# Whole background tiles between the steps of the scans' chain

## The reference, cut to what matters

```python
def chunk_scan(q, k, v, log_a):          # S_t = diag(a_t) S_{t-1} + k_t v_t^T, o_t = S_t^T q_t
    def step(state, inp):
        qc, kc, vc, ac = inp
        cum = jnp.cumsum(ac, axis=2)
        o_inter = jnp.einsum('bhtk,bhkv->bhtv', qc * jnp.exp(cum), state)
        diff = cum[:, :, :, None, :] - cum[:, :, None, :, :]
        decay = jnp.where(causal_in_chunk, jnp.exp(jnp.where(causal_in_chunk, diff, 0.0)), 0.0)
        scores = jnp.einsum('bhtk,bhsk,bhtsk->bhts', qc, kc, decay)
        o_intra = jnp.einsum('bhts,bhsv->bhtv', scores, vc)
...
def bidir_scan(q, k_fwd, k_bwd, v, la_fwd, la_bwd):
    fwd = chunk_scan(q, k_fwd, v, la_fwd)
    bwd = flip(chunk_scan(flip(q), flip(k_bwd), flip(v), flip(la_bwd)))
    return (fwd + bwd).astype(q.dtype)
...
o_b = mixer_hgrn2(b_q, b_ff, b_fb, b_i, b_g, lower_bounds[l], hgrn_norm_g[l])
o_c = mixer_gla(c_q, c_k, c_v, c_g, c_lrf, c_lrb, gla_gate_w2[l], gla_gate_b[l], gla_norm_g[l])
g_a, g_b, g_c = jnp.split(jax.nn.sigmoid(gates), N_BRANCH, axis=-1)
```

## Time and profile before

| | us |
|---|---|
| median of 3 runs | 5423.82 |
| lowest, highest run | 5412.58, 5428.38 |
| profiled execution, time | 5412.35 |
| profiled execution, span | 5410.8 |
| TensorE (PE) busy in the span | 4449.6 (82%) |
| VectorE (DVE) busy | 2012.1 (37%) |
| ScalarE (ACT) busy | 1194.3 (22%) |

### The profile page before, as it was taken

The page is one execution under the profiler, slowest core; times in us unless marked ns, Lnnn a source line. Parts: engine busy times, 40 slices in busy tenths (PEclk is TensorE's granted clock), DMA queues, the critical chain, the costliest instruction groups (busy, mean ns, idle before and its releaser), DMA issues. The chain is left out here.

```text
span 5410.8 us, 54373 instructions
## 1 busy us (share of the span) xinstructions
PE 4449.6 (82%) x20668; PEld 2944.3 (54%) x20668; DVE 2012.1 (37%) x3485; ACT 1194.3 (22%) x2000; POOL 274.2 (5%) x450
## 2 busy tenths in 40 slices
PE   6999998666689699996598997399778877973995
PEld 2365643444444588885397873344356766733442
DVE  0266630333352555554233751400133366514011
ACT  0123310222220100001113751011134424510111
POOL 0000000000000000000031000011000000000111
PEclk9899999888899799998799998599899989985997
DMA  7101211000021311112223113199500012120996
GB/s 307 51 27 54 72 70 77 19 19 19 0 94 66 125 47 47 47 47 117 96 67 121 37 44 117 41 326 335 171 3 4 2 44 105 42 109 32 321 334 206
DMA packets 104466, 521.96 MB, mean 96 GB/s; under 512 B 15825, under 2 KB 37217, under 8 KB 84593
## 3 DMA queue, kind: packets, MB, share of 16 engines
q1 hardware_dynamic: 70752, 404.86, 20.1%
q0 software_dynamic: 30432, 112.81, 6.5%
q10 hardware_dynamic: 3120, 2.10, 0.1%
HBM read 438.46 MB, written 81.26 MB: 96 GB/s over the span
## 5 line engine op out<-in xcount | busy, mean ns | idle before, releaser
L1700 PE MATMUL scans_G<-ring,hT 128*128 128x512 f32 (+1 forms) x1024 | 394.5, 543 | 6.2 <-ACT scans_stg L1818 6.2
L1700 PEld LDWEIGHTS scans_G<-ring,hT 128*128 128x128 f32 x1024 | 192.8, 191 | 193.5 <-issue 176.0
L2199 PE MATMUL moe_g_ps<-ring,moe_xT 128*128 128x512 f32 x512 | 229.6, 602 | 3.0 <-ACT moe_xT L2253 1.5
L2235 PE MATMUL moe_y_ps<-ring,moe_aT 128*128 128x512 f32 x512 | 225.2, 593 | 1.5 <-issue 1.5
L2199 PE MATMUL moe_u_ps<-ring,moe_xT 128*128 128x512 f32 x512 | 225.0, 592 | 0.0
L153 PE MATMUL mlp_z<-ring_r,mlp_w_high 128*128 128x512 f32 x512 | 200.7, 392 | 22.1 <-DVE ring_r L147 22.0
L154 PE MATMUL mlp_z<-hT_r,mlp_w_high 128*128 128x512 f32 x512 | 199.8, 390 | 0.0
L155 PE MATMUL mlp_z<-ring_r 128*128 128x512 f32 x512 | 199.7, 390 | 0.0
L153 PE MATMUL mlp_y_ps<-mlp_w_high,oN_r 128*128 128x512 f32 x512 | 199.2, 389 | 0.0
L154 PE MATMUL mlp_y_ps<-ring_r,oN_r 128*128 128x512 f32 x512 | 199.2, 389 | 0.0
L155 PE MATMUL mlp_y_ps<-mlp_w_high,oN_r 128*128 128x512 f32 x512 | 199.2, 389 | 0.0
(11 more groups left out here) (499 smaller groups left out, 8672.4 us busy)
## 6 DMA issues: line engine op xcount, KB each, us to landing
ring<-in_w_all SPq DMA_DIRECT2D x126, 2048.0 KB, 8.3
ring<-in_w_mlp SPq DMA_DIRECT2D x16, 2048.0 KB, 7.5
branch_gates<-scans_stg POOLq DMA_DIRECT2D x48, 256.0 KB, 2.3
merge_raw<-branch_gates SPq DMA_DIRECT2D x16, 768.0 KB, 5.2
ring<-in_w_even SPq DMA_DIRECT2D x6, 1536.0 KB, 8.6
norm_moe_x<-x_rows SPq DMA_DIRECT2D x16, 512.0 KB, 7.4
h_rows<-norm_moe_h POOLq DMA_DIRECT2D x16, 512.0 KB, 2.9
diff_w<-in_w_diff POOLq DMA_DIRECT2D x4, 1536.0 KB, 6.6
```

The costliest lines, as they stand in the source:

```text
L1700: ins = pe.matmul(G[:, b % 2, 0:w.shape[2]], m["hT"][:, k, n * P:(n + 1) * P], w[:, k, :], start=k == 0, stop=k == KD - 1)
L2199: ins = pe.matmul(what[:, j % 2, :], xT[:, j % 2, k, :], w[:, k, :], start=k == 0, stop=k == KD - 1)
L2235: ins = pe.matmul(Y[:, half, :], aT[:, j % 2, k, :], w[:, k, half * HALF:(half + 1) * HALF], start=k == 0, stop=k == K4 - 1)
```

## The change

The condition of the loop in `background` is changed. Before, a matmul was put out as long as the background put out so far was less than `us`, so that a call could stop in the middle of a tile. Now a tile that has been started is always finished (`at[1]` is not 0), and a new one is started only if at least half of its cost lies before `us`.

```diff
             def background(us):
 
-                while at[0] < len(TILES) and at[2] < us - 1e-6:
+                while at[0] < len(TILES) and (at[1] or at[2] + 0.5 * COST[TILES[at[0]][0]] < us):
                     b, k = at[0], at[1]
                     what, x, j, n = TILES[b]
                     w = wview(j)
```

## The result

| | before | after |
|---|---|---|
| median, us | 5423.82 (5 runs) | 5453.94 (5 runs) |
| lowest, highest | 5412.58, 5428.38 | 5447.49, 5463.84 |
| ratio of the times, with its 95% interval | | 1.006 (1.0042 to 1.0077) |
| profiled execution, us | 5412.35 | 5459.52 |

The change makes the kernel 30.1 us slower; 5445 was forecast, 21 us slower. The stage, from its first matmul (L1716) to the end of the tail, lasted 732.9 us before and 770.1 after in the profiled executions: 37.2 us more, of their difference of 47.2. The other 10 us lie in stages whose code is the same; executions of one kernel differ by as much.

A forecast was written before the change was run, and what follows sets the result against it. The prediction took TensorE's work plus its idle time to bound the stage. Added idle time of 16.3 us and 5.1 for the clock gave +21.4 on the median of 5423.82, so 5445 us, range 5426 to 5460.

The forecast's parts named there:

- What bounds the stage: End of the scans' stage: TensorE's work plus its idle time; the chain's own length counts for nothing else.
- The lengths of the levels without the clock: Turn 0's eight levels: sum 107.1 us instead of 95.76, so 11.4 us longer.
- The wait ahead of level 1: Turn 0, empty second window of level 0: TensorE waits 5 us before level 1.
- Idle time of 13.1 us in turn 0 and 16.3 in the stage: TensorE's added idle time: 13.1 us in turn 0's levels, 0.9, 1.6 and 0.7 elsewhere in the stage.
- Behind the turns: Between turns: 0.86 us more idle behind turn 0; net +0.7 behind turn 1, where TensorE arrives about 1.2 early.
- The level 4 wait of turn 1: Turn 1, level 4: a lone N tile leaves TensorE 1.6 us idle where none was.
- The clock: Turn 0's levels: three clock falls, one in level 0 and two at 2.8 us gaps, 1.7 us each: +5.1 (0 to +12).
- the third of the rivals: Turn 0: clock falls at nearly every empty window, some seven times 1.7 us; +28 us, 5452; chance 0.20.
- a gain from uncut tiles: Turn 0's levels: pauses come from restarting after cut tiles, about 14 of 15.8 us idle go; 5410; chance 0.04.
- The change is not hidden by ScalarE: Rival for the stage: ScalarE's planned copies hold TensorE, so time stays at 5424 within 5; chance 0.04.
- The clock didn't stay up: Rival for turn 0: clock stays up, +16.3 us or up to 3 less, 5437 to 5440; chance 0.16.
- The total: Whole kernel: 16.3 us without the clock plus 5.1 for the clock, +21.4 us, 5445 against the median.

The follow-up runs named there:

- overfull: Kernel before with 4 and 7 matmuls instead of 2 and 5 planned into turn 0's first and second windows: 5413.42 us against 5423.23.
- filled_more: Changed kernel with useless matmuls in turn 0's empty windows and behind lone N tiles of second windows: 5437.78 us against 5423.23 for the kernel before.
- turns12_whole: Kernel before with whole tiles only in turns 1 and 2, turn 0 as before: 5424.56 us against 5421.59.
- turn0_whole: Kernel before with whole tiles only in turn 0, turns 1 and 2 as before: 5456.17 us against 5421.59.
- tile_per_window: Changed kernel replanned so each window of turn 0's levels gets exactly one tile, with ScalarE's copies and later starts adjusted: 5432.41 us against 5422.66 for before.
- first_empty: Kernel before with all first windows of turn 0 empty, their background moved to the second ones, no whole tiles: 5459.91 us against 5421.59.
- one_empty: Kernel before with only the first window of level 3 in turn 0 empty, its background moved to the second: ratio 1.0011 to before.
- level0_empty: Kernel before with both windows of level 0 in turn 0 empty, the background moved to level 1's first window: ratio 1.0017 to before.
- whole_filled: Changed kernel with useless matmuls in the windows of turn 0 that it leaves empty: 5451.71 us against 5421.59 for the kernel before.
- tuned: Kernel before with 3 and 6 matmuls instead of 2 and 5 planned into turn 0's first and second windows: 5414.15 us against 5422.66.

## Why the prediction was nearly right, point by point

**What bounds the stage**: right. The end is TensorE's work plus its idle time; overfull (levels 14.8 us longer, stage 10.1 shorter) shows it more strongly than any row of before did.

**The lengths of the levels without the clock**: right. Levels 4 and 5, where the clock stays at 1.00, last 12.82 us each for the 12.79 worked out. The predicted sum of 107.1 came out at 109.48 when the windows were filled. The wait ahead of level 1 was said to be 5 us and is 4.97. Idle time of 13.1 us in turn 0 and 16.3 in the stage stands: it is the larger part of the 20.1 us that filled_more keeps, and with the 19.3 and 1.6 us below it makes up the stage's 37.2.

**Behind the turns**: right in sizes that hardly matter. The wait for ScalarE behind turn 0 is 6.02 us, 0.85 more than in the earlier trace rows (0.86 predicted). The other two, from TensorE's timeline after:

```profile
589.72 2.06 PE L1780 MATMUL scans_A<-scans_KQ 64*128 64x128 f32 x32 [1.54 <-DVE scans_KQ L2050]
...
666.61 2.23 PE L1744 MATMUL scans_A<-identity,scans_E 128*128 128x128 f32 x16 [1.32 <-DVE scans_E L1964]
```

The level 4 wait of turn 1 is 1.54 us (1.6 predicted) and the one behind turn 1 is 1.32 (1.2 predicted), at a transpose. The wait of 0.48 us at 628.76 is gone, as predicted.

**The clock**: the step that failed, in size. Counted level by level against the prediction, turn 0 is longer by

| level | 0 | 1 | 2 | 3 | 4 | 5 | 6 | 7 |
|---|---|---|---|---|---|---|---|---|
| predicted, us | 11.89 | 16.21 | 13.85 | 11.95 | 12.79 | 12.79 | 13.82 | 13.82 |
| measured, us | 13.61 | 20.72 | 17.54 | 13.67 | 12.82 | 12.82 | 18.09 | 17.13 |

which sums to 19.3 us, all of it in rows at the low clock. The term was 3 x 1.7 = 5.1, with 12 as its upper bound, and 19.3 lies beyond that bound too. It failed in both factors. The falls are five, not three: level 0 and each of the levels 2, 3, 6 and 7, so all four gaps of 2.8 us and not two. And a fall costs 3.9 us on average, not 1.7: 6.2 for levels 0 and 1 together, 3.7, 1.7, 4.3 and 3.3 for the others. Level 3 is the cheapest, since its slow N tile runs into time that would have been idle. The 1.7 came from the earlier trace rows, where gate tiles of 7 us follow one another without a pause and the clock returns in under 4 us. Here what follows is a group of 2 us and often another gap, and the clock stays low for 6 to 20 us. The row was a right witness that the clock falls and a wrong one for how long. That the work behind the gap makes the difference is argued, not shown: no run puts a long tile straight behind a gap of 2.7 us. The kernel came out near the third of the rivals, which gave +28 us with the remark that slow groups may add to it; measured are +30.1 by the medians, and +37.2 in the stage of the profiled pair. Its factors were off as well: seven falls at 1.7 us, where five at 3.9 were found.

In the stage some 1.6 us are left over: a fall of its own behind the prologue of turn 0, where a product of keys and values takes 3.45 us behind a wait of 2.48. The same wait is in before without a fall. TensorE's timeline before, then after:

```profile
312.75 1.97 PE L1757 MATMUL scans_B<-scans_V,scans_KQ 128*128 128x256 f32 x8 [2.48 <-DVE oN L1975]
...
315.65 3.45 PE L1757 MATMUL scans_B<-scans_V,scans_KQ 128*128 128x256 f32 x8 [2.48 <-DVE oN L1975]
```

The fall stands in the profiles of all five kernels whose prologue holds 32 matmuls, and in one of the seven with 29: turns12_whole, whose order up to there is that of before. So the changed prologue may favour this fall, but isn't needed for it, and its cause stays open. The prediction gave the prologue no price.

The Trainium skill, "TensorE: Matmul & The Clock Gate", section "HAM oscillation — how this bites in real kernels", says that gaps between bursts bring the half level back and that each return costs again. This trace agrees: each of the six gaps of 2.7 us and more in the levels of turn 0 was followed by a group of 2.97 to 3.79 us instead of 2.05. In the forecast I weighed it with the full clock of the earlier trace rows, which stands beside pauses of under 1.4 us and so said nothing of gaps of 2.7. The row at 312.75 above, a wait of 2.48 us at full clock, was nearer; the prediction didn't use it, and it would have pointed the wrong way.

**The refuted rivals**: a gain from uncut tiles doesn't exist; where nothing stands between two groups the second still starts 2.70 us behind the end of the first, which is the selection's time. The change is not hidden by ScalarE either. The clock didn't stay up.

**The total** came near with one term far too small and nothing to make up for it: 16.3 held, and the clock's 5.1 should have been some 14 (30.1 less 16.3) by the medians and 19.3 by the profiled execution. The profiled execution, 5459.52, is 5.6 us above the median of its kernel, and the one of before 11.5 below its own, so the stage's figures lean to the high side. How much the falls vary from run to run was not measured, but turn0_whole is a second sample of the same order in turn 0: its levels last 127.21 us at 0.77, with a fall in level 5 that the kernel after doesn't show and a shorter one in level 6.

## What to carry to other kernels

Where one engine bounds a stage and fills the gaps of a chain, count the time that it stands idle, not the length of the chain: too much in a gap cost nothing on balance here (overfull was 0.15% faster, though its waits for ScalarE's copies rose by 2.3 us), too little costs its length once. Here it cost about as much again through TensorE's clock, at gaps of some 2.7 us between small groups, so price such a gap from a row with the same work around it, not from one between long tiles. If filler must be rounded to whole pieces, rounding up in every gap did better here than rounding to the nearest piece (tile_per_window against after), but it was still 0.16% slower than cut pieces.

## What the runs showed of the hardware

- While groups of 16 matmuls with 32 rows and 128 columns alternated with gaps of 2.8 and 5 us, the clock did not come back: 0.50 from 340 to 360 us in the kernel after. Each fall in its levels lasted 6 to 20 us, against under 4 in the earlier trace rows.
- Every gap of 2.69 us or more ahead of a group in the levels of turn 0 came with a fall: 23 of 23 in after, turn0_whole, first_empty, one_empty and level0_empty, with groups of 2.59 to 3.79 us instead of 2.05. The wait of 2.48 us ahead of L1757 came with one in six profiles of twelve.
- A pause of 1.3 to 1.5 us behind an N tile of 256 columns was followed by a fall in whole_filled (392.97, 411.08, 423.59) and in tile_per_window (353.99, 372.09, 384.61), and by none in levels 4 and 5 of the kernel after (415.79, 428.61), where the rows around it read the same. In turn0_whole, with the same order as after, both of these pauses were followed by slow rows (417.93, 430.45). In these four kernels it is eight of fourteen such pauses. What decides it is open.
- The wait of 1.32 us ahead of the first group was followed by a fall where the wait of 2.48 us had been followed by one, 24 us earlier (turns12_whole, whole_filled, filled_more, tile_per_window), and by none where it had not (before, one_empty, overfull, tuned). These are the kernels with work straight behind that group. What ties the two together is open.
- With pauses of up to 0.9 us between the same groups the clock stayed at 1.00 through all levels of turn 0 in before.
- A changeover between kinds of matmul took 0.18 us, also where nothing waits: 16 of them are in turn 0's levels, and no plan that puts background into every window removes them.
